# Two transformer-like blocks on one core: Fourier halves joined on VectorE, first weight pieces loaded a stage ahead, a pass change done tile by tile

## The reference

```python
def first_block(x, ...):
    h = rmsnorm(x, norm1_g);  proj = h @ w_in
    y = concat([hyena_mixer(proj[..., :1536], ...), fourier_mixer(proj[..., 1536:])])
    x = x + head_rmsnorm(y, mix_g) @ w_out
    h = rmsnorm(x, norm2_g)            # group by argmax, two experts of that group, softmax weights
    x = x + sum_over_two(weight * (silu(h @ w_gate[e]) * (h @ w_up[e])) @ w_down[e])
    return rmsnorm(x, final_g)

def fourier_mixer(u):                  # per group of 64 channels
    return fftn(u, axes=(sequence, channel), norm='ortho').real

def second_block(x, ...):
    q, k, v, u, gates = split(rms_norm(x, norm_mix_pre) @ w_in)
    g_a, g_b = split(sigmoid(gates + b_gate))
    mix = (g_a * (band_attention(q, k, v, rel_bias) @ w_attn_out) + g_b * (pool(u) @ w_pool_out)) @ w_o
    x = x + rms_norm(mix, norm_mix_post)
    val, gate = split(causal_conv3(rms_norm(x, norm_ffn_pre) @ w_up))
    return x + rms_norm((gelu(gate) * val) @ w_down, norm_ffn_post)
```

## Time and profile before

| | us |
|---|---|
| median of three runs | 2731.07 (2730.14 to 2733.98) |
| the profiled execution, whole | 2730.56 |
| its span in the profile | 2728.8 |
| TensorE busy | 2426.1 (89%) |
| VectorE busy | 1604.5 (59%) |
| ScalarE busy | 1059.6 (39%) |
| GpSimd busy | 455.5 (17%) |

### The profile page before, as it was taken

The page is one execution under the profiler, slowest core; times in us unless marked ns, Lnnn a source line. Parts: engine busy times, 40 slices in busy tenths (PEclk is TensorE's granted clock), DMA queues, the critical chain, the costliest instruction groups (busy, mean ns, idle before and its releaser), DMA issues. The chain is left out here.

```text
span 2728.8 us, 28252 instructions
## 1 busy us (share of the span) xinstructions
PE 2426.1 (89%) x11032; PEld 1838.3 (67%) x11032; DVE 1604.5 (59%) x1703; ACT 1059.6 (39%) x1268; POOL 455.5 (17%) x297
## 2 busy tenths in 40 slices
PE   5799985994999999991899989998979999988998
PEld 1378742783666666661777768886768888876777
DVE  5533285526999999976310562222478999873344
ACT  1311112223777777763211662111344443432332
POOL 3200312001222222211310120000024233310000
PEclk7899997896999999995899989999989999998999
DMA  3011114118999999975311011111322222217443
GB/s 136 16 55 46 41 43 149 54 77 311 364 382 382 389 382 379 377 296 207 101 46 56 1 40 47 46 46 56 121 66 84 84 86 93 78 39 245 144 128 131
DMA packets 191840, 397.19 MB, mean 146 GB/s; under 512 B 16022, under 2 KB 119574, under 8 KB 175336
## 3 DMA queue, kind: packets, MB, share of 16 engines
q1 hardware_dynamic: 182504, 378.76, 38.9%
q0 software_dynamic: 9216, 16.80, 1.9%
HBM read 357.75 MB, written 47.18 MB: 148 GB/s over the span
## 5 line engine op out<-in xcount | busy, mean ns | idle before, releaser
L1449 DVE TENSOR_TENSOR expert_rest<-expert_raw,expert_high 128x2048 fp32r<-128x2048 f32 x124 | 281.0, 2290 | 32.1 <-ACT expert_high L1443 30.7
L141 PE MATMUL up_ps<-blocks_high,up_operand_high 128*128 128x512 f32 x616 | 240.9, 391 | 12.4 <-DVE up_operand_rest L3102 12.4
L1443 ACT ACTIVATE expert_high<-expert_raw 128x2048 fp32r<-128x2048 f32 x124 | 236.8, 1913 | 18.9 <-PE expert_up_ps L143 8.4
L143 PE MATMUL up_ps<-blocks_high,up_operand_rest 128*128 128x512 f32 x616 | 240.7, 391 | 0.0
L1449 DVE TENSOR_TENSOR expert_rest<-res,expert_high 128x2048 fp32r<-128x2048 f32 x68 | 154.5, 2290 | 18.9 <-ACT expert_high L1443 18.4
L141 PE MATMUL down_ps<-w_down_high,prod_high 128*128 128x512 f32 x352 | 139.5, 396 | 26.2 <-DVE w_down_rest L181 18.6
L1804 POOL DMA_INDIRECT expert_rows<-y_rows,out_ids x32 | 84.0, 2625 | 427.1 <-DVE y_rows L1761 427.1
L3102 DVE TENSOR_TENSOR up_operand_rest<-res,up_operand_high 128x512 fp32r<-128x512 f32 x154 | 144.4, 949 | 3.4 <-ACT up_operand_high L3057 3.4
L3015 POOL TENSOR_TENSOR res<-res 128x512 f32<-128x512 f32 x22 | 37.7, 1714 | 633.7 <-POOLq L2727 406.4
L141 PEld LDWEIGHTS up_ps<-blocks_high,up_operand_high 128*128 128x128 f32 x616 | 116.4, 189 | 36.8 <-DVE up_operand_rest L3102 12.8
L142 PE MATMUL down_ps<-w_down_rest,prod_high 128*128 128x512 f32 x352 | 138.6, 394 | 0.0
(11 more groups left out here) (400 smaller groups left out, 6070.4 us busy)
## 6 DMA issues: line engine op xcount, KB each, us to landing
expert_raw<-in_w_gate_dram SPq DMA_DIRECT2D x42, 1024.0 KB, 15.7
expert_raw<-in_w_down_dram SPq DMA_DIRECT2D x42, 1024.0 KB, 17.0
expert_raw<-in_w_up_dram SPq DMA_DIRECT2D x40, 1024.0 KB, 16.6
res<-in_w_in_dram SPq DMA_DIRECT2D x48, 512.0 KB, 4.1
res<-in_w_up_dram SPq DMA_DIRECT2D x24, 1024.0 KB, 16.9
res<-in_w_down_dram SPq DMA_DIRECT2D x22, 1024.0 KB, 18.5
res<-in_w_gate_dram SPq DMA_DIRECT2D x22, 1024.0 KB, 18.4
res<-in_w_up_dram SPq DMA_DIRECT2D x88, 256.0 KB, 4.0
```

The costliest lines, as they stand in the source:

```text
L141: nc.tensor.matmul(out, w_high, x_high, start=start, stop=False)
L143: return nc.tensor.matmul(out, w_rest, x_high, start=False, stop=stop)
L1443: self.nc.scalar.activation(self.high_part[:, n % SPLIT_SLOTS, :], self.raw[n % RAW_SLOTS], ACT.Copy) \
L1449: self.nc.vector.tensor_tensor(self.rest_part[:, s, :], self.raw[n % RAW_SLOTS], self.high_part[:, s, :].bitcast(F32), ALU.subtract).then_ ...
```

## The change

Five edits, in order of time:

1. *Join.* The two 128x2048 instructions of the join leave GpSimd and stand on VectorE, behind the whole filter chain (after the last `v_done`) and ahead of the first scaling of the back transform.
2. *Routing.* `rows` is now made before `route`; there GpSimd blanks it and issues the first three gathers as soon as `row_ids` is there. ScalarE splits the high parts of the first weight units in `route`, VectorE one rest. In `experts` every engine reads the count of extra blocks at the start; GpSimd no longer waits for its scatters. That wait, with a read of the count, stands on SyncE in `combine`, and the load of the final gamma comes after the first two loads of rows.
3. *First pieces.* The first two gate pieces are loaded into `m.res` by SyncE during `band_attention`; the first two of w_o at the end of `gated_mix`; the first three steps of the down projection in the last step of `ffn_up`, before the store of the last product. To free `m.res` for these the last residual gets a buffer of its own in `ffn_down`.
4. *Residual.* In `mix_output` the load of the whole residual (4 MB) into `m.res` waits until all eight pieces of w_o have been split, as the raw pieces now lie in it.
5. *Change of pass.* The last three steps of the first pass are done tile by tile, as those of the second were. ScalarE and VectorE let tiles 0 to 2 leave PSUM before they split step 22, tile 3 after step 23.

The core of the diff:

```diff
@@ -985,9 +984,6 @@
             for c in range(HT):
                 nc.gpsimd.tensor_scalar(m.zT[:, c, :], m.zT[:, c, :], col(m.params, "f_bias", c), None, ALU.mult) \
                     .then_inc(bias_done, 1)
-            pool.wait_ge(four_kept, 2 * HT + 1)
-            nc.gpsimd.tensor_tensor(given[:, :, 0:HALF], four_low, four_high, ALU.add)
-            nc.gpsimd.tensor_tensor(given[:, :, HALF:SEQ], four_low, four_high, ALU.subtract)
...
+            given = m.mixT[:, HT:2 * HT, :]
+            dve.wait_ge(four_kept, 2 * HT + 1)
+            nc.vector.tensor_tensor(given[:, :, 0:HALF], four_low, four_high, ALU.add)
+            nc.vector.tensor_tensor(given[:, :, HALF:SEQ], four_low, four_high, ALU.subtract)
...
+        @block.gpsimd
+        def _(pool):
+            nc.gpsimd.memset(rows.data[:], 0.0).then_inc(rows.blank, 1)
+            pool.wait_ge(rows.blank, 1)
+            pool.wait_ge(ids_done, 1)
+            for b in range(rows.SLOTS):
+                rows.take(pool, b, m.row_ids[:, b:b + 1])
...
+            for n in range(SPLIT_SLOTS - 1):
+                weights.high(act, n)
...
+            weights.rest(dve, 0)
             dve.wait_ge(list_mm, 1)
...
-            nc.gpsimd.memset(rows[:], 0.0).then_inc(rows_set, 1)
-            pool.wait_ge(rows_set, 1)
-            for b in range(R):
-                gather(b)
+            count = over_count(pool)
...
-            for s in range(S):
-                pool.wait_ge(y_out[s], 16 * (EXPERTS // S))
...
-            count = over_blocks(pool, over)
-            pool.wait_ge(y_out[0], (count + EXPERTS // S) * 16)
-            pool.sem_inc(waited_pool, 1)
+            over_blocks(pool, count, over)
...
+            count = over_count(dve)
+            weights.rest(dve, 1)
             x_in(0)
-            for n in range(SPLIT_SLOTS - 1):
+            for n in range(2, SPLIT_SLOTS - 1):
                 weights.rest(dve, n)
...
-            sp.dma_start(g_row[:], A["final_g"].to_broadcast([P, D])).then_inc(g_in, 16)
+            count = sp.value_load(m.over_table[0:1, OVER:OVER + 1], min_val=0, max_val=OVER)
+            sp.wait_ge(m.y_out[1], 16 * (EXPERTS // 2))
+            sp.wait_ge(m.y_out[0], (count + EXPERTS // 2) * 16)
+            sp.sem_inc(waited_rows, 1)
             for t in range(TT):
+                if t == 1:
+                    sp.dma_start(g_row[:], A["final_g"].to_broadcast([P, D])).then_inc(g_in, 16)
...
+        @block.sync
+        def _(sp):
+            for s in range(2):
+                at = (4 * ATT // P + s * KT) * P
+                sp.dma_start(m.gates_raw[s], A["w_in_2"][0].rearrange("(k p) n -> p k n", p=P)[:, :, at:at + P]) \
+                    .then_inc(m.gates_in[s], 16)
...
+            for k in range(2):
+                sp.wait_ge(ring.rest_done[k], KT)
+                sp.dma_start(m.w_o_raw[k], A["w_o_2"][0, k * P:(k + 1) * P, :]).then_inc(m.w_o_in[k], 16)
...
+            sp.wait_ge(wide.w_rest, KT)
             sp.dma_start(m.res[:], m.res_dram.rearrange("(t p) d -> p t d", p=P)).then_inc(norm.res_in, 16)
...
+                if f == FT - 1:
+
+                    sp.wait_ge(rest_done, len(PLAN))
+                    sp.wait_ge(sums_done, 4 * FT)
+                    for i in range(2):
+                        sp.wait_ge(stored[i], 16 * (FT // 2 - 1))
+                    for n in range(pieces.SLOTS):
+                        pieces.load(sp, n)
...
-            for n in range(N):
-                f, s = n % FT, n % S
-                if n >= S:
-                    sp.wait_ge(x_rest_done, n - S + 1)
-                here = slice(n // FT * QUAD * P, (n // FT + 1) * QUAD * P)
-                sp.dma_start(x_raw[:, s, :], m.prod_dram[f, :, here]).then_inc(x_in[s], 16)
-                ring.load(sp, n % S, n // S, A["w_down_2"][0, f * P:(f + 1) * P, :], first=(n < S))
+            for n in range(S, N):
+                sp.wait_ge(x_rest_done, n - S + 1)
+                sp.wait_ge(ring.rest_done[n % S], n // S)
+                pieces.load(sp, n)
                 if n == S:
                     sp.dma_start(norm.gamma[:], A["norm_ffn_post_2"].to_broadcast([P, D])).then_inc(norm.gamma_in, 16)
...
-            for n in range(N - S):
-                ready(n)
+            for turn in range(2):
+                for n in range(turn * FT, (turn + 1) * FT - S):
+                    ready(n)
+                    for q in range(QUAD):
+                        products(n, q)
+
                 for q in range(QUAD):
-                    products(n, q)
-
-            for q in range(QUAD):
-                for n in range(N - S, N):
-                    if q == 0:
-                        ready(n)
-                    products(n, q)
+                    for n in range((turn + 1) * FT - S, (turn + 1) * FT):
+                        if q == 0:
+                            ready(n)
+                        products(n, q)
...
         def _(act):
+            def leave(t):
+                tile_done(act, t)
+                norm.scalar_part(nc, act, m, t, ps[:, t % QUAD, :, :])
+
             for n in range(N):
+                if n == FT:
+
+                    for t in range(QUAD - 1):
+                        leave(t)
                 if n >= S:
                     act.wait_ge(ring.used[n % S], n // S)
                 act.wait_ge(x_in[n % S], 16 * (n // S + 1))
-                nc.scalar.activation(x_high[:, n % S, :], x_raw[:, n % S, :], ACT.Copy).then_inc(x_high_done, 1)
+                nc.scalar.activation(x_high[:, n % S, :], x_raw[n % S], ACT.Copy).then_inc(x_high_done, 1)
                 ring.high(act, n % S, n // S, first=(n < S))
-                if n == FT + S - 1:
-
-                    for t in range(QUAD):
-                        tile_done(act, t)
-                        norm.scalar_part(nc, act, m, t, ps[:, t, :, :])
+                if n == FT + 1:
+                    leave(QUAD - 1)
             for t in range(QUAD, TT):
-                tile_done(act, t)
-                norm.scalar_part(nc, act, m, t, ps[:, t % QUAD, :, :])
+                leave(t)
 
         @block.vector
         def _(dve):
             for n in range(N):
+                if n == FT:
+                    for t in range(QUAD - 1):
+                        norm.vector_part(nc, dve, m, t, ps[:, t, :, :])
                 dve.wait_ge(x_high_done, n + 1)
-                nc.vector.tensor_tensor(x_rest[:, n % S, :], x_raw[:, n % S, :], x_high[:, n % S, :].bitcast(F32), ALU.subtract) \
+                nc.vector.tensor_tensor(x_rest[:, n % S, :], x_raw[n % S], x_high[:, n % S, :].bitcast(F32), ALU.subtract) \
                     .then_inc(x_rest_done, 1)
                 ring.rest(dve, n % S, n // S)
-                if n == FT + S - 1:
-                    for t in range(QUAD):
-                        norm.vector_part(nc, dve, m, t, ps[:, t, :, :])
+                if n == FT + 1:
+                    norm.vector_part(nc, dve, m, QUAD - 1, ps[:, QUAD - 1, :, :])
```

144 lines of the change are left out of this document (83 added, 61 removed).

## The result

The changed kernel has a median of 2701.89 us (2696.64 to 2705.6, four runs) against 2731.05: ratio 0.989, 95% interval 0.9872 to 0.9908. Forecast were 2703 and 2691 to 2714. The profiled execution took 2702.13 with a span of 2700.3, so the spans differ by 28.5. The table cuts both spans at the first product behind each wait of TensorE; its columns are differences of start times in the two timelines. A row is named by the product that ends it, so the products of `ffn_up` themselves lie in the row *down projection*, and both passes of the down projection in the last row. One execution of experiment 3 took 3659.51 us at a mean granted clock of 0.642 and is left out of every number.

What follows compares the result with a forecast made beforehand. TensorE has the most work, so only its gaps, some 300 us, can shrink. Terms 8.6 + 0.7 + 3.0 + 4.2 - 0.4 + 4.1 + 7.5 = 27.7 off 2730.56 give 2702.9, forecast 2703 us, range 2691 to 2714.

Steps and rivals of the forecast that it cites:

- Join: Before the back transform: without GpSimd's join VectorE's slow pair of sums speeds up, join hidden on VectorE; gain 8.6 us.
- Start of the experts: Routing to first expert product: gathers end earlier, but leaving the block then takes GpSimd 6.8 us; gain 0.7 us.
- End of the experts: Into combine: GpSimd leaves right behind its last scatter, SyncE waits for the landing and loads earlier; gain 3.0 us.
- Gates: Start of gated_mix: first gate pieces already loaded, so TensorE starts earlier; gain 4.2 us.
- w_o and the residual: mix_output: TensorE starts 2.2 us earlier, but the residual's later load sets the end; loss 0.4 us.
- Down pieces: Start of the down projection: first pieces already loaded, so TensorE starts earlier; gain 4.1 us.
- Change of pass: Between the down projection's passes: tile-by-tile steps lose 2.5 us in place of 10.0; gain 7.5 us.
- R1: Rival: leaving a block waits for the DMAs' landing; experts' start -3.6, end 0, time 2710 us; chance 25%.
- R2: Rival: leaving a block is nearly free; 6.6 and 6.5 us at experts' start and end, time 2693.5; chance 12%.
- R3: Rival: slow pair has another cause or join isn't hidden; 4 to 8.6 us less gain, 2707 to 2711; 7%.
- R4: Rival: kernel slower, barrier between gathers and experts holding GpSimd over 33 us; at 40 us 2737; chance 2%.
- The case of no difference: Pieces no earlier, pass gain lost elsewhere, only the join left and the barrier at 20 us; about 2728 us; 3%.

Runs made afterwards that it cites:

- experiment 3: Kernel before with only the last three steps of each down-projection pass done tile by tile; 2726.21 us, ratio 0.9976.
- 2: Kernel before with only the join moved from GpSimd to VectorE behind the filter chain; 2721.62 us, ratio 0.9965.
- 4: Changed kernel with the first three gathers issued at the start of the expert stage again, blanking left beside the routing; 2695.01 us, ratio 0.9864.
- 5: Changed kernel with GpSimd again waiting for the landing of its scatters before leaving the expert stage; 2701.7 us, ratio 0.9893.
- 7: Changed kernel with the final gamma loaded in the expert stage, into a free slot of the weight stream; 2697.65 us, ratio 0.9872.
- 10: Changed kernel with the first two gate pieces loaded at the start of gated_mix again; 2706.12 us, ratio 0.9899.
- 1: Changed kernel run again without any edit, for spread and a second profile; 2703.23 us, ratio 0.9896.
- 9: Changed kernel with the third tile's residual sum placed behind the rests of step 22; 2698.22 us, ratio 0.9883.
- 11: Changed kernel with gathers in the expert stage, two tiles' rows and gamma loaded early, third tile's sum behind step 22's rests; 2691.2 us, ratio 0.985.
- 12: Changed kernel with gathers in the expert stage, six tiles' rows early, gamma late, third tile's sum behind step 22's rests; 2700.27 us, ratio 0.989.

## Why the prediction was right

The sum was 27.7 and the spans differ by 28.5; by its own steps:

- **Join**, 8.6: 8.3, and shown alone (2). The cause, the pair of sums beside GpSimd's additions, is confirmed. Left out: 1.1 us in the next stretch, of which 0.7 to 0.8 are time at half clock that goes with the gap (2); in 3, without this edit, that stretch is as before.
- **Start of the experts**, 0.7: 1.9. The failing term is the 6.8 us for leaving a block, which I took from a stretch that also held a count's read on GpSimd: from the last gather instruction it is 4.8 to SyncE's load and 5.8 to the turn here, for which I had put the 6.8. The blanking beside the routing chain cost nothing: TensorE's two waits for that chain are 11.2 and 12.3 us in both kernels. That the barrier eats most of the gain was right, and 4 shows what it costs: 3.4 us more are had by not gathering there.
- **End of the experts**, 3.0: 3.0, but as the difference of two terms. The first load comes 3.2 us earlier (forecast 2.9, and 5 confirms it), the first sum 5.5, as its rows no longer stand behind the gamma; but 2.4 are given back at the second tile, where I had put 0.3 for the gamma in all (7).
- **Gates**, 4.2: 4.0 in its stretch, 4.3 alone (10).
- **w_o and the residual**, -0.4: +1.9. The load alone took 12.9 us; I had scaled 14.3 from one that shared the queue. So the residual landed 0.8 us earlier in its block than before; the other 1.1 lie in the gates' products and are the clock's spread (10).
- **Down pieces**, 4.1: 5.4. From SyncE's store of the last product to TensorE's first product it is 10.6 before and 6.0 after, so 4.6, as much as TensorE's wait fell (18.36 to 13.76). The other 0.8 is the clock at the start of `ffn_up`, 0.84 over the first 10 us of products for 0.74 before. In the second profile of the same kernel the wait is the same 13.8 us and this row saves only 0.6 (1).
- **Change of pass**, 7.5: 5.7. The wait was 1.97 for 2.25. The half clock behind it, which I had left to the lower bound, came in this profile and in a third of those with this wait (3).
- **Rows put at nothing.** The row *`ffn_up`* lost 1.4, which is the clock behind the norm (1); the expert stage lost 0.7, within the 563.0 to 564.3 us that it takes over all 14 profiles.

R1 (25%) falls by 5, R2 (12%) by the rows of both barriers, R3 by 2. R4's barrier of 33 us is 4.8. The case of no difference doesn't add up as written: a join of 8.6 against a barrier of 20 us, 13.2 more than the 6.8 of the sum, gives no gain by the sum's own terms but about 2734, not 2728. The misses of single terms, up to 2.3 us, went both ways; that the sum came out within 1.1 us of the median is part luck: the four runs alone span 9 us, and the clock, for which the sum had no term at the start of a stage, gave about 0.7, 1.1 and 0.8 in three rows and took 1.4 and 1.6 in two others.

What stays open: what decides in an execution whether the clock falls behind a wait of 2 us and how soon it is back at the start of a stage, and which of the two courses VectorE and GpSimd take in `ffn_up`.

## What to carry to other kernels

Ask of an instruction that is moved ahead of a barrier what that engine's leave then costs: a gather issued early in the block before was later than one issued at once in its own. What is queued in front of a needed load counts: a gamma of half a MB between two tiles' rows cost 2.4 us, twelve issues ahead of a barrier with the gamma behind them 5.6. And where executions spread by 3 to 9 us, read an effect of 3 us from its stretch of the profile, not from the median.

## What the runs showed of the hardware

- A block in which GpSimd issued indirect DMAs was left 4.8 us (gathers) and at most 6.45 us (scatters, with SyncE's read of the count) behind its last DMA instruction, landing or not; where GpSimd waited for the landing first, that wait came on top (5). Only the scatters tell this from a wait for the landing: they had landed 3.5 us before SyncE's first load, the third gather 0.4 us before it (landings of 3.9 and 5.5 us behind the start). With no such DMA in it the block was left within 0.4 us, and GpSimd's DRAIN right behind a blanking took 0.03 us (4).
- VectorE and GpSimd with two float32 inputs each, side by side, have two courses: in one GpSimd's 128x512 addition stood open for 10.59 us and VectorE kept its times, in the other it took 3.17 and VectorE's subtractions 1.77 for 0.68 and 3.37 for 2.28. By the Trainium skill, page *SBUF — State Buffer*, section *Who interferes with whom*, the order of issue decides which of the two blocks. That they hold each other up these rows bear out; the order they don't show, as the recorded starts are the same to 0.02 us in both courses. The second course cost 1.93 us of wait and 1.7 at half clock behind it, of the 4.8 us between the two executions (1).
- Behind a wait of 1.97 us TensorE's granted clock fell to its lower level (1.2 of 2.4 GHz) in three of nine profiles (0.72 in the mean over 2568 to 2574 us of the changed kernel's); behind one of 0.71 us it stayed up in all three (9, 11, 12). Behind the waits of 1.6 to 1.95 us in `ffn_up` it fell in two of five (1). A fall behind the change of pass cost 1.6 us.
